# A two-block transformer on one core: weight residuals queued sooner, one-column matmuls spread over eight blocks, first weights fetched ahead of x

## The reference

```python
# first_block: two layers (windowed attention, then a gated linear recurrence), each followed by an MLP
x = x + concatenate([mixed, memory_attention(mq, mk, mv)]) @ w_out[l]
x = x + square(relu(rms_norm(x, mlp_norm[l]) @ w_up[l])) @ w_down[l]
# then rms_norm(x, final_norm), and second_block on it
mod = silu(c) @ w_ada + b_ada            # 3 x 1024 numbers: shift, scale, gate
h = rmsnorm(x, norm_g) * (1 + scale) + shift
proj = h @ w_in                           # queries, keys, values, gates
# stick-breaking attention and sliding-window attention, each times silu(gate)
x = rmsnorm(x + gate * (concatenate([y_sb, y_sw]) @ w_out), final_g)
```

## Time and profile before

| | |
|---|---|
| median of 3 runs | 3200.7 us |
| profiled execution, its own time | 3196.59 us |
| its span | 3194.8 us |
| PE busy | 3080.3 us, 96% |
| DVE busy | 1696.2 us, 53% |
| ACT busy | 1105.6 us, 35% |
| mean granted PE clock | 0.989 |

### The profile page before, as it was taken

How to read it: one execution, slowest core, us unless ns; L and a number is a source line. 1 busy time by engine, 2 the same in 40 slices (tenths; PEclk the granted TensorE clock), 3 DMA queues, 4 the chain that set the end, 5 groups by cost and what they waited for, 6 DMA issues and landing times. The chain is left out here.

```text
span 3194.8 us, 34615 instructions
## 1 busy us (share of the span) xinstructions
PE 3080.3 (96%) x14262; PEld 2387.1 (75%) x14272; DVE 1696.2 (53%) x2173; ACT 1105.6 (35%) x1723; POOL 89.9 (3%) x70
## 2 busy tenths in 40 slices
PE   8999999999999999999999999999999999999888
PEld 7885567788888888777777888888887687666566
DVE  7737854544444433589854633333333734656575
ACT  4215632311111111387732311111111515776552
POOL 0004510000000000000000000000000000000000
PEclk9999999999999999999999999999999999999999
DMA  4320011122222211211131111111111131000213
GB/s 148 114 94 1 1 73 34 53 80 66 67 79 73 73 47 47 86 47 47 54 124 34 47 47 46 47 53 46 47 47 46 53 124 35 20 21 20 93 39 121
DMA packets 54510, 190.96 MB, mean 60 GB/s; under 512 B 6288, under 2 KB 6672, under 8 KB 54224
## 3 DMA queue, kind: packets, MB, share of 16 engines
q1 hardware_dynamic: 54352, 188.74, 18.0%
HBM read 172.73 MB, written 14.68 MB: 59 GB/s over the span
## 5 line engine op out<-in xcount | busy, mean ns | idle before, releaser
L285 PE MATMUL PS<-H,wsp 128*128 128x512 f32 x6864 | 1613.8, 394 | 38.7 <-DVE wsp L141 16.5
L285 PEld LDWEIGHTS PS<-H,wsp 128*128 128x128 f32 x6864 | 1290.6, 189 | 347.1 <-issue 40.1
L285 PE MATMUL PS<-p,wsp 128*128 128x512 f32 (+1 forms) x3840 | 895.2, 393 | 20.7 <-DVE p L141 20.7
L285 PEld LDWEIGHTS PS<-p,wsp 128*128 128x128 f32 x3840 | 711.3, 189 | 198.6 <-ACT wsp L138 21.5
L138 ACT ACTIVATE p<-p 128x1024 f32<-128x1024 f32 (+7 forms) x426 | 361.3, 872 | 861.6 <-DVE p L144 678.6
L138 ACT ACTIVATE wsp<-raw 128x1024 fp32r<-128x1024 f32 (+1 forms) x267 | 276.9, 1040 | 698.3 <-PE PS L285 490.9
L141 DVE TENSOR_TENSOR p<-p,PS 128x1024 f32<-128x1024 f32 (+2 forms) x232 | 244.4, 1054 | 496.5 <-PE PS L285 496.5
L141 DVE TENSOR_TENSOR wsp<-raw,wsp 128x1024 fp32r<-128x1024 f32 (+1 forms) x267 | 321.8, 1207 | 159.4 <-ACT wsp L138 152.4
L141 DVE TENSOR_TENSOR p<-PS,p 128x1024 f32<-128x1024 f32 (+2 forms) x116 | 131.0, 1130 | 371.8 <-PE PS L285 346.9
L141 DVE TENSOR_TENSOR p<-p 128x1024 fp32r<-128x1024 f32 (+5 forms) x239 | 239.6, 1010 | 114.8 <-ACT p L138 111.6
L285 PE MATMUL PS<-p 128*64 128x256 f32 (+9 forms) x1432 | 283.9, 464 | 12.7 <-ACT p L138 3.0
(11 more groups left out here) (70 smaller groups left out, 1051.4 us busy)
## 6 DMA issues: line engine op xcount, KB each, us to landing
raw<-in_in_dram SPq DMA_DIRECT2D x72, 512.0 KB, 3.5
raw<-in_dn_dram SPq DMA_DIRECT2D x65, 512.0 KB, 3.5
raw<-in_up_dram SPq DMA_DIRECT2D x64, 512.0 KB, 3.5
raw<-in_out_dram SPq DMA_DIRECT2D x42, 512.0 KB, 3.5
p<-in_ada_dram SPq DMA_DIRECT2D x24, 512.0 KB, 4.4
p<-in_x_dram SPq DMA_DIRECT2D x16, 512.0 KB, 7.3
raw<-in_kv_dram SPq DMA_DIRECT2D x16, 512.0 KB, 3.5
spill_dram<-p SPq DMA_DIRECT2D x16, 512.0 KB, 2.9
```

The lines of the kernel that those rows point to most:

```text
L285: return pe(lambda e: e.matmul(o, l, r, start=start, stop=stop, **kw), *a)
```

## The change

It has four edits.

1. SP fetches weight block 0 ahead of chunk 0 of x. ACT and DVE do split(0), prepare of chunk 0, split(1), square of chunk 0.
2. The 24 one-column matmuls leave group 7 of the first MLP. `mod_step` runs behind each of the eight down blocks of group 6: it takes a pair, queues three of them, and a DVE instruction writes three columns of `modT`.
3. After the first `two_blocks`, split of b0+9 is called before the first `scaled_x` and `next_mod` of the high half.
4. In `one_more`, for n = 0, split of b0+10 is called before the copy and `next_mod` of chunks 3 and 4.

```diff
         X0 = place(8 * KB, [128, 8, 1024])
+        load(0)
         xload = [Q.dma(None, X0[:, 0, :], D["x"][:, 0, :])]
-        load(0)
         load(1)
...
         for k in range(8):
-            prepare(k, X0[:, k, :], V("mix_norm0", k), xload[k])
-            st.add(k, X0[:, k, :], xload[k])
             if k == 0:
                 split(0)
+            prepare(k, X0[:, k, :], V("mix_norm0", k), xload[k])
+            if k == 0:
                 split(1)
+            st.add(k, X0[:, k, :], xload[k])
...
+                    if g == 6 and beside:
+                        beside(n)
                     if g == 7:
                         last_evac(n, xl[n], last["up"], last["U"])
...
-            if n == 1:
-                pp = take_pair()
-                for j in range(24):
-                    q = mm(PS[:, 2 * pp, j:j + 1], acc[:, j // 8, (j % 8) * 128:(j % 8) * 128 + 128], ones[:, 0:1], True, True,
-                           free[2 * pp], ada["acc"])
-                ada["mod"] = TT(modT[:, :], PS[:, 2 * pp, 0:24], V("b_ada", 0, 24), ALU.add, q)
-                free[2 * pp] = [ada["mod"]]
...
+        def mod_step(n):
+            pp = take_pair()
+            for j in range(3 * n, 3 * n + 3):
+                q = mm(PS[:, 2 * pp, j - 3 * n:j - 3 * n + 1], acc[:, j // 8, (j % 8) * 128:(j % 8) * 128 + 128],
+                       ones[:, 0:1], True, True, free[2 * pp], ada["acc"])
+            ada["mod"] = TT(modT[:, 3 * n:3 * n + 3], PS[:, 2 * pp, 0:3], V("b_ada", 3 * n, 3), ALU.add, q)
+            free[2 * pp] = [ada["mod"]]
+
+        mlp(0, st, after0, ada_step, mod_step)
...
         def one_more(n, p, ps, op):
+            if n == 0:
+                split(at[0] + 2)
             o = A(SQ[:, 2 + n, 0:512], ps, ACT.Copy, op, up1)
...
         split(at[0] + 1)
+        split(at[0] + 2)
         box["x"] = scaled_x(0, 1, up1)
```

More of the change, by code:

```diff
@@ L927, in norm_of, with mlp @@
             return R, finish(st, R, buf(64), buf(76), buf(68))
-        def mlp(l, st, last_evac, extra=None):
+        def mlp(l, st, last_evac, extra=None, beside=None):
             U = place(32 * KB, [128, 2, 4, 1024], F32R)
@@ L1098, in after0 @@
             st1[0].add(n, X[:, n, :], o)
-        mlp(0, st, after0, ada_step)
+        def mod_step(n):
[6 more added lines that the diff above has]
+        mlp(0, st, after0, ada_step, mod_step)
         mod_ready = ada["mod"]
```

## The result

The changed kernel takes 3185.59 us (median of five runs, 3184.82 to 3187.8), the kernel before on the same chip 3200.01 (3198.16 to 3201.22). The ratio is 0.9961, with a 95% interval of 0.9949 to 0.9972: 12.5 us less, between 9.0 and 16.3 (14.4 by these two medians alone). The forecast was 10.1 less. The profiled execution of the changed kernel took 3187.80 with a span of 3186.0, that is 8.8 less than the profiled one of before. The two profiles give a smaller difference than the medians, since before's profiled execution, at 3196.59, was shorter than all five timed here, and after's was the longest of its five.

The account below looks back on a forecast made before the run. PE, busy 96% of the span, was taken as the bound; -5.9 - 1.7 - 3.0 + 1.0 - 0.5 = -10.1 us took the median from 3200.7 to 3190.6, range 3186.8 to 3197.0.

Parts of the forecast that it names:

- Queries: At the query blocks, earlier weight residuals shorten PE's waits by 3.9 us and avoid a clock fall worth 2.0: 5.9 together.
- Rival 1: DVE and ACT set the key and value stage's end, so the queries' 5.9 us are lost there; 3196.5, chance 0.10.
- One-column matmuls: In the first MLP, spreading them over group 6 leaves their work equal and removes the clock fall behind them: 1.7 us.
- Rival 3: The clock falls at each of the eight one-column groups, 1.7 us each, making the kernel slower; 3204.2, chance 0.05.
- Banks: The shifted pair counter wins 3.0 us at the last projection and costs 1.0 at layer 1's output projection.
- rival 2: The last projection still waits, held by something else from DVE's chain, so its 3.0 us are lost; 3193.6, chance 0.12.
- Start: With weight block 0 fetched first, PE starts at 8.9 instead of 9.46; 0.5 us taken, between -0.3 and 2.2.
- rival 4: More than forecast: the clock's rise at the start comes early, or layer 1's projection costs nothing; 3188, chance 0.07.
- (b): Layer 1's output projection gets pair 3 instead of pair 0 and waits for bank 7's addition: costs 1.0 us.

Follow-up runs that it names:

- pairs_back: The changed kernel with one more take_pair call behind the first MLP, so every later stage has the kernel before's bank pair; 3187.28 us, ratio 0.9967.
- pairs_only: The kernel before with three more take_pair calls behind the first MLP, so every later stage has the changed kernel's bank pair; 3197.14 us, ratio 1.0003.
- undo_queries: The changed kernel with the early splits of both b0+9 and b0+10 undone; 3190.79 us, ratio 0.9980.
- edit3_only: The changed kernel with b0+10's split put back behind chunks 3 and 4, b0+9's split still early; 3194.81 us.

## Why the prediction was right, and where its sizes were off

**Queries: right in mechanism and size.** 5.9 forecast, 5.87 in the stage; one idle of 1.18 for the forecast 1.2, a clock of 1.00 behind it, and PE going on 9.98 after b0+8's residual began, where the prediction's own times (2549.00 and 2539.02) made it 9.98. What it had wrong is inside the term: it walked through edit 3 first, as if that were a step of the gain, and edit 4 alone gives all of it. Its reason for a clock of 1.00 behind the idle, that none fell behind the 2.93 at the last projection, was weaker than it looked, since `pairs_back` has a fall behind the same idle. The outcome itself is steady: none of the six profiles with one idle of 1.18 to 1.23 here has a fall behind it, and all four with one of 4.1 have (before, `pairs_only`, `undo_queries`, `edit3_only`).

**Rival 1 is refuted.** Had the chain of DVE and ACT set the end of that stage, it would have taken 5.9 us back before the stop behind the values. The stage is 5.87 shorter, counted up to that stop.

**One-column matmuls: right mechanism, mis-sized term.** The work sums to nothing as forecast. The clock's part was put at 1.7, from the one fall that before's trace shows. Where the batch stands undivided the fall cost 1.6, 3.1 and 3.2 in three executions, 2.6 on average. One profile gives one draw of such a fall, not its mean.

**Rival 3 is refuted** by nine profiles of eight groups each, all within 0.06 us of each other (205.75 to 205.81), without a row near 0.5. The Trainium skill's rule in "TensorE: Matmul & The Clock Gate", "A second HAM failure mode: psum-queue depth-cycling", that small idles between groups make the clock go up and down, isn't put to the test by the one-column groups, which leave no idle; the 0.81 idle that each group of down blocks has (the one ahead of group 6 among them) is followed by the full clock after the change as it was before, where no long batch stands behind it.

**Banks: right.** The last projection gained 3.0 as forecast, and the additions from banks 6 and 7 run beside it; `pairs_back` brings the idle back and `pairs_only` takes it out of the kernel before, so rival 2 is refuted. Layer 1's projection cost the 1.0 of the sum, 6.92 - 5.89 by the starts of PE's matmuls; the idle itself is 0.87 (the prediction called it "about 0.6" in one place).

**Start: right on average, not in the profile.** PE begins at 8.90 as said, and the 0.56 that this wins is lost again until the statistics (33.56 for 33.49). Over thirteen profiles the edit gives some 0.5 to 0.7. How much the start varies by itself is shown by the ten profiles with the edit, which run the same program up to the statistics: from PE's first matmul to there they take 23.2 to 24.7 us. The Trainium skill's rule that was cited for this, in "TensorE: Matmul & The Clock Gate", part 1, says that the monitor runs free of the kernel's start; the traces agree in this much, that the same start comes out differently from one execution to the next.

**The 2.4 us beyond the forecast.** The forecast of 10.1 less lies inside the interval of both measurements (9.0 to 16.3, and 9.9 to 17.9). As a time, the median of 3185.59 is 1.2 below the range that was given, against a kernel before that stood at 3200.01 here and not at 3200.7; 0.9961 of 3200.7 is 3188.2, inside the range and next to rival 4's 3188. Neither of rival 4's reasons is seen in the profile, though: (b) costs its 1.0, and the statistics begin no earlier. Three things can make up the difference. The batch's fall costs 0.9 more on average than was put down; the stretch up to the first MLP's first down group is 2.1 shorter on average in the ten profiles with edit 1 than in the three without, of which the forecast has 0.5; and two executions of one kernel differ by up to 4 us through falls in stages that no edit touches. How much of the 2.4 belongs to each can't be told: it is less than the measurement resolves.

## What to carry to other kernels

Where an engine waits for one thing made in order by another, count the instructions ahead of the last one that it needs. An edit that only re-orders what stands ahead wins at most an overlap (here 1.05 of the 3.9). A counter that hands out banks or buffers in turn ties distant stages together: an edit that calls it one time more or fewer moves waits a thousand microseconds away, 3.0 us off one place and 1.0 on another, and an edit that skips three of four at once makes the next block wait for the pair in use (1.41 us of idle in two kernels). So walk the counter through the whole program before and after. And when a term rests on a fall of the clock, read it from several executions, or give it a range as wide as the falls that one trace shows in different places.

## What the runs showed of the hardware, unexpected

- A batch of one-column matmuls makes the granted clock fall, though PE has no idle time directly ahead or within: 48 in a row (as the trace counts them; 5.4 to 6.5 us) did in three of three kernels, 24 in 2.7 us in one of two places, 6 in 0.72 us in none of 72 (nine kernels, eight groups each).
- The same idle time at the same place, 2.93 and 2.94 us ahead of the last projection, was followed, 1.5 us later, by the lower level in `pairs_back` (0.51 for 3.5 us) and not in before. At the half blocks an idle of 2.92 us was followed by it in twelve of the thirteen profiles.
- The length of a fall at one and the same place differs between executions of like work: behind the same wait one block of 24 matmuls took 7.15 us at a mean clock of 0.79 and 8.62 at 0.65, and the first matmuls of the half blocks, 23 in 6.7 us at 0.75 in one kernel, were 17 at 0.55 in another. Time of this kind belongs to no edit.
